# S5 mixer: the first input unit multiplied token block by token block, the last unit's halves in two banks, and the first gate products ahead of the second output turn

## The reference, cut to what matters

```python
def second_block(x, ...):
    for i in range(2):
        h = rmsnorm(x, mix_pre_gain[i])
        m = fox_mixer(h, ...) if i == 0 else s5_mixer(h, ...)
        x = x + rmsnorm(m, mix_post_gain[i])
        h = rmsnorm(x, ffn_pre_gain[i])
        x = x + rmsnorm(swiglu(h, ...), ffn_post_gain[i])

def s5_mixer(h, w_in, ..., d_skip, w_glu, w_out):
    u = h @ w_in                       # 1024 x 1024
    # u -> 64 groups of 16 channels, complex diagonal recurrence over the tokens,
    # in chunks; y = C x, summed over 64 states a group
    y = y + d_skip * u
    y = gelu(y)
    y = y * sigmoid(y @ w_glu)         # 1024 x 1024
    return y @ w_out
```

## Time and profile before

| | us |
|---|---|
| median of 3 runs | 989.36 (989.02 to 989.72) |
| the profiled execution's own time | 988.04 |
| its span | 986.2 |
| PE busy in it | 963.3 (98%) |
| DVE busy | 583.5 (59%) |
| ACT busy | 506.9 (51%) |
| POOL busy | 310.8 (32%) |

### The profile page before, as it was taken

One profiled execution on the slowest core, in us unless ns is written; L12 is line 12 of the kernel. 1 busy time (PEld: TensorE's weight loads), 2 busy tenths in 40 slices (PEclk: granted clock), 3 DMA queues, 4 the chain that ended last, 5 costly groups with the idle time before them and its releaser, 6 DMA issues.

```text
span 986.2 us, 14283 instructions
## 1 busy us (share of the span) xinstructions
PE 963.3 (98%) x5446; PEld 800.2 (81%) x5446; DVE 583.5 (59%) x639; ACT 506.9 (51%) x723; POOL 310.8 (32%) x331
## 2 busy tenths in 40 slices
PE   8999999999999989999999999999989999999997
PEld 6977777888888868888888888888978888888886
DVE  4898875554554456565774545546586755545544
ACT  6855465444443467456654444434456564444332
POOL 5670447999699216763010000000000020000000
PEclk9999999999999999999999999999999999999999
DMA  9842026676776746545446657557946456557551
GB/s 335 271 136 86 1 90 220 224 224 222 264 230 225 223 147 212 162 164 171 129 147 199 187 173 241 185 206 247 381 167 215 128 173 197 185 172 254 172 170 43
DMA packets 133827, 186.79 MB, mean 189 GB/s; under 512 B 5904, under 2 KB 104720, under 8 KB 133264
## 3 DMA queue, kind: packets, MB, share of 16 engines
q1 hardware_dynamic: 109632, 158.28, 49.3%
q10 hardware_dynamic: 24144, 27.81, 8.2%
HBM read 174.54 MB, written 15.73 MB: 193 GB/s over the span
## 4 chain that ended last, share of the span: by engine, by line
PE 91%; DVE 5%; ACT 2%; issue 1%; POOL 0%; DVEq 0%; POOLq 0%; ACTq 0%
PE ps L510 25%; PE ps L482 16%; PE ps L484 16%; PE ps L483 16%; PE ps L1055 2%; PE ps L462 2%; PE ps L464 2%; PE ps L463 2%; PE ps L839 1%; PE ps L1631 1%; PE ps L1074 1%; DVE wlo L422 1%; PE ps L1065 1%; PE ps L621 1%; PE ps L1160 1%
## 5 line engine op out<-in xcount | busy, mean ns | idle before, releaser
L422 DVE TENSOR_TENSOR wlo<-wraw,whi 128x2048 fp32r<-128x2048 f32 x127 | 302.0, 2380 | 293.1 <-ACT whi L416 293.1
L416 ACT ACTIVATE whi<-wraw 128x2048 fp32r<-128x2048 f32 x127 | 243.2, 1915 | 255.4 <-PE ps L484 156.3
L482 PE MATMUL ps<-whi,actH 128*128 128x512 f32 x640 | 258.0, 403 | 6.8 <-DVE wlo L422 5.9
L484 PE MATMUL ps<-whi,actL 128*128 128x512 f32 x640 | 250.2, 391 | 0.0
L483 PE MATMUL ps<-wlo,actH 128*128 128x512 f32 x640 | 249.4, 390 | 0.0
L482 PEld LDWEIGHTS ps<-whi,actH 128*128 128x128 f32 x640 | 120.3, 188 | 33.7 <-DVE wlo L422 6.5
L484 PEld LDWEIGHTS ps<-whi,actL 128*128 128x128 f32 x640 | 120.1, 188 | 26.1
L756 POOL TENSOR_SCALAR ss<-ss 128x1 f32<-128x1 f32 x8 | 1.8, 221 | 436.1 <-ACT sg L726 436.1
L483 PEld LDWEIGHTS ps<-wlo,actH 128*128 128x128 f32 x640 | 120.5, 188 | 22.3
L510 PE MATMUL ps<-whi,gH 128*128 128x512 f32 x248 | 77.8, 393 | 0.0
L510 PE MATMUL ps<-wlo,gH 128*128 128x512 f32 x248 | 76.8, 390 | 0.0
(11 more groups left out here) (452 smaller groups left out, 1573.7 us busy)
## 6 DMA issues: line engine op xcount, KB each, us to landing
wraw<-in_ffn_w_gate SPq DMA_DIRECT2D x44, 512.0 KB, 4.0
wraw<-in_ffn_w_up SPq DMA_DIRECT2D x44, 512.0 KB, 4.9
wraw<-in_ffn_w_down SPq DMA_DIRECT2D x18, 1024.0 KB, 4.9
wraw<-in_fox_w_in SPq DMA_DIRECT2D x16, 1024.0 KB, 5.4
wraw<-in_w_gate SPq DMA_DIRECT2D x22, 512.0 KB, 4.1
wraw<-in_w_up SPq DMA_DIRECT2D x22, 512.0 KB, 5.0
wraw<-in_w_in SPq DMA_DIRECT2D x9, 1024.0 KB, 11.2
wraw<-in_w_down SPq DMA_DIRECT2D x9, 1024.0 KB, 5.0
```

The costliest lines, as they stand in the source:

```text
L416: act.activation(self.high_of(n0), self.wraw[:, n0 % RAW, :], ACT.Copy).then_inc(self.hi_done, 1)
L422: dve.tensor_tensor(self.low_of(n0), self.wraw[:, n0 % RAW, :], self.high_of(n0).bitcast(F32), ALU.subtract).then_inc(self.lo_done, 1)
L482: pe.matmul(out, xh, wh, start=(ka == 0), stop=False)
L484: last = pe.matmul(out, xl, wh, start=False, stop=(ka == KT - 1))
```

## The change

Four places, all in the S5 layer's code:

- The first input unit takes the activations as the stationary operand and the weights as the moving one (`mm_tokens`), first for row block 0, then for row block 1. The turn of `x_res` becomes the row-by-row turn that the feed-forward parts already use (`pe_row_turn`, `act_row_turn`, `dve_row_turn`), and the 40 matmuls on the identity go. The unit's result has tokens on partitions; ACT copies it into `sg`, and PE turns it back with four transposes in the middle of the second unit. Its low part now lies in its raw slot, so the first gate unit's transfer waits for `used` of this unit.
- The fourth input unit puts its first half of features in bank 3 and its second half in bank 0, so that DVE can take the first half while PE computes the second.
- `turn_inputs(0)` turns all of `Vc` first and then all of `Vs`, each behind its own wait.
- The first gate unit's products with the first tile are issued ahead of `turn_outputs(1)`; ACT's gelu table load moves ahead of `states_swapped(3)`, its order around `outputs_out(3)` and DVE's around `yg_low` change.

Semaphores of the first layer's LayerNorm are renamed (`ln_total`), with the same waits.

```diff
-        self.early_low = {f["s"]: early["b"], f["f2.down"] + FT // 2 - 1: early["act"]}
+        self.early_low = {f["f2.down"] + FT // 2 - 1: early["b"]}
...
+    def mm_tokens(self, pe, st, n0, r, bank):
+        pe.wait_ge(self.lo_done, n0 + 1)
+        out = self.ps[:, bank, r * 256:(r + 1) * 256]
+        for k in range(KT):
+            pe.wait_ge(*self.past(st + "_act_ready", KT * r + k + 1))
+            wh, wl = (t[:, k * 256:(k + 1) * 256] for t in (self.high_of(n0), self.low_of(n0)))
+            xh, xl = self.actH[:, k, r * P:(r + 1) * P], self.actL[:, k, r * P:(r + 1) * P]
+            pe.matmul(out, xh, wh, start=(k == 0), stop=False)
+            pe.matmul(out, xh, wl, start=False, stop=False)
+            last = pe.matmul(out, xl, wh, start=False, stop=(k == KT - 1))
+        if r == RT - 1:
+            last.then_inc(self.used, 1)
...
-            m.pe_ffn(pe, "f2", f2_turn, last_units=2, half=lambda: s_first(0), end=lambda: s_first(1))
-            s_rest()
-            for i in range(4):
-                m.mm_features(pe, first["s"] + i, i, ready="s_act_ready" if i == 0 else None,
-                              late=late if i == 0 else None)
+            s_turn = lambda r, part: m.pe_row_turn(pe, "s", "pf0_x_ready", ROWS_HIGH, r, part)
+            m.pe_ffn(pe, "f2", f2_turn, last_units=2, half=lambda: s_turn(0, 0), end=lambda: s_turn(0, 1))
+            m.mm_tokens(pe, "s", first["s"], 0, 0)
+            s_turn(1, 0)
+            s_turn(1, 1)
+            m.mm_tokens(pe, "s", first["s"], 1, 0)
...
+            for i in range(1, 4):
+                if i == 3:
+                    pe.wait_ge(*m.past("ut1", 1))
+                m.mm_features(pe, first["s"] + i, i, middle=tokens_turned if i == 1 else None,
+                              second=0 if i == 3 else None)
...
-            turn_outputs(1)
             n = first["glu"]
             pe.wait_ge(m.lo_done, n + 1)
             for i, k in enumerate(Y_ORDER):
+                if i == 1:
+                    turn_outputs(1)
                 pe.wait_ge(*m.past("yg_act_ready", i + 1))
+                if i == 0:
+                    pe.wait_ge(*m.past("y_out_a", 3))
                 for f in range(2):
-                    o, c = ps[:, 3 * f, 0:TOK], k * 256 + f * P
+                    o, c = ps[:, 2 * f, 0:TOK], k * 256 + f * P
...
-            for i in range(4):
+            for i in range(3):
                 m.act_post_square(act, "pf0", 0, "f2_first", n, i)
+            m.act_row_turn(act, "s", ROWS_HIGH, 0, range(4), MIXPRE + 8)
+            m.act_post_square(act, "pf0", 0, "f2_first", n, 3)
+            m.act_row_turn(act, "s", ROWS_HIGH, 0, range(4, KT), MIXPRE + 8)
             act.wait_ge(*m.past("pf0_squares", 2 * RT))
             act.dma_start(m.RTab[:], m.Rd).then_inc(sem("r_in"), 16)
+            m.act_row_turn(act, "s", ROWS_HIGH, 1, range(KT), MIXPRE + 8)
             act.wait_ge(*m.past("pf0_normed", 2 * RT))
             act.dma_start(m.gb[1][:], io["ffn_post_gain_2"][1:2, :].to_broadcast([P, D])).then_inc(sem("gain1_in"), 16)
-            m.act_turn(act, "s", (4, 5, 6, 7, 2, 3), gain=MIXPRE + 8)
             for r in range(RT):
                 m.act_pre_square(act, "s", "pf0_x_ready", r)
+            act.wait_ge(m.used, n + 1)
+            act.activation(m.sg[:], ps[:, 0, :], ACT.Copy).then_inc(sem("s_tokens"), 1)
...
+            act.activation(m.nmax[:, 0, 0:1], m.halfpi[:], ACT.Gelu_apprx_tanh)
             states_swapped(3)
-            act.activation(m.nmax[:, 0, 0:1], m.halfpi[:], ACT.Gelu_apprx_tanh)
             outputs_out(2)
...
             for i in range(4):
-                dve.wait_ge(m.used, n + i + 1)
                 for h in range(2):
-                    dve.tensor_tensor(m.uT[:, h, :, i, :],
-                                      ps[:, i, h * TOK:(h + 1) * TOK].rearrange("p (c t) -> p t c", t=T),
+                    if i == 0:
+                        dve.wait_ge(*m.past("s_features", 1))
+                    elif (i, h) == (3, 0):
+                        dve.wait_ge(*m.past("features_half", 1))
+                    else:
+                        dve.wait_ge(m.used, n + i + 1)
+                    src = ps[:, 0, 0:TOK] if (i, h) == (3, 1) else ps[:, i, h * TOK:(h + 1) * TOK]
+                    dve.tensor_tensor(m.uT[:, h, :, i, :], src.rearrange("p (c t) -> p t c", t=T),
                                       by_step, ALU.mult).then_inc(sem(f"ut{h}"), 1)
...
-                if i == 3:
-                    yg_low(0)
-                    yg_low(1)
-                if i > 3:
+                if i > 1:
                     yg_low(i - 2)
```

More of the change, by code:

```diff
@@ L106, in resolve @@
             counts["ao"] = counts["fo"] = KT // 2
-            for s in ("f1", "fp", "f2", "f3"):
+            for s in ("f1", "fp", "f2", "s", "f3"):
                 counts[s] = RT * KT
@@ L349, in place @@
             ("gain", self.where["postgain0"]), ("nat", self.where["nat"]), ("c", R0 + 36864), ("a", R0 + 49152),
-            ("b", R0 + 57344), ("d", self.where["Uall"]), ("qt", self.where["qt1"]),
-            ("act", self.where["actL"]))}
+            ("b", R0 + 57344), ("d", self.where["Uall"]), ("qt", self.where["qt1"]))}
         self.junk1 = at("junk1", [P, D], F32, self.where["qn"])
@@ L447, in low_piece, with mm_features @@
                           ALU.subtract).then_inc(done, 1)
-    def mm_features(self, pe, n0, bank, it=0, ready=None, order=range(KT), middle=None, late=None):
-        pe.wait_ge(self.lo_done, n0 + 4 * it + 1)
+    def mm_features(self, pe, n0, bank, order=range(KT), middle=None, second=None):
+        pe.wait_ge(self.lo_done, n0 + 1)
         high, low = self.high_of(n0), self.low_of(n0)
@@ L454, in mm_features @@
             out = self.ps[:, bank, f * TOK:(f + 1) * TOK]
+            if second is not None and f == 1:
+                last.then_inc(self.sem("features_half"), 1)
+                out = self.ps[:, second, 0:TOK]
             for i, k in enumerate(order):
[L456 to L459, removed]
                 c = k * 256 + f * P
@@ L640, in dve_row_turn @@
                .then_inc(self.sem(st + "_act_ready"), 1)
[L642 to L672, removed]
     def pe_spread(self, pe, st, bank):
@@ L1858, in turn_inputs @@
             def turn_inputs(b):
[L1860 to L1865, removed]
+                parts = ((m.Vc, b, 3 + b),) if b > 0 else ((m.Vc, 0, 1), (m.Vs, 4, 3))
+                for src, bank, ready in parts:
+                    pe.wait_ge(*m.past("vc_a", ready))
+                    for q in range(4 * b, 4 * b + 4):
+                        last = pe.transpose(ps[:, bank, (q % 4) * P:(q % 4 + 1) * P], src[:, q, :], idn[:])
                 last.then_inc(sem("v_turned"), 1)
@@ L2286, in _, with yg_gelu, yg_high @@
             outputs_out(1)
+            act.activation(m.nmax[:, 0, 0:1], m.halfpi[:], ACT.Gelu_apprx_tanh)
             states_swapped(3)
-            act.activation(m.nmax[:, 0, 0:1], m.halfpi[:], ACT.Gelu_apprx_tanh)
             outputs_out(2)
-            for i, kt in enumerate(Y_ORDER + (None,)):
-                if i == 2:
-                    outputs_out(3)
-                if kt is not None:
-                    act.wait_ge(*m.past("y_sum", i + 1))
-                    act.activation(m.ygT[:, kt, :], m.ygT[:, kt, :], ACT.Gelu_apprx_tanh).then_inc(sem("gelu"), 1)
-                if i > 0:
-                    act.wait_ge(*m.past("gelu", i))
-                    act.activation(m.actH[:, Y_ORDER[i - 1], :], m.ygT[:, Y_ORDER[i - 1], :], ACT.Copy)\
-                       .then_inc(sem("yg_high_ready"), 1)
+            def yg_gelu(i):
+                yg = m.ygT[:, Y_ORDER[i], :]
+                act.wait_ge(*m.past("y_sum", i + 1))
+                act.activation(yg, yg, ACT.Gelu_apprx_tanh).then_inc(sem("gelu"), 1)
+            def yg_high(i):
+                kt = Y_ORDER[i]
+                act.wait_ge(*m.past("gelu", i + 1))
+                act.activation(m.actH[:, kt, :], m.ygT[:, kt, :], ACT.Copy).then_inc(sem("yg_high_ready"), 1)
+            for i in range(2):
+                yg_gelu(i)
+                yg_high(i)
+            outputs_out(3)
+            for i in range(2, KT):
+                yg_gelu(i)
+                if i > 2:
+                    yg_high(i - 1)
+            yg_high(KT - 1)
             n = first["glu"]
```

27 lines of the change are left out of this document (17 added, 10 removed), and 2 rows, old and new, of the table KINDS.

## The result

The changed kernel took 997.99 us (median of 6 runs, 997.25 to 1000.84), the kernel before 989.54 us beside it. The ratio is 1.0087, 95% interval 1.0073 to 1.0101. My 988.5 us and my range of 986.9 to 989.9 were both wrong.

A forecast was written before the change was run, and what follows sets the result against it. PE was taken to bound the input units, DVE the recurrence. Profiled 988.04 less 0.87 + 0 + 0.3, plus 0.34, gave 987.2; the same 0.83 off the median 989.36 gave 988.5 us, range 986.9 to 989.9.

The forecast's parts named there:

- Part 4: End of the recurrence: first gate products ahead of the second output turn, table load moved earlier; a loss of 0.34 us.
- part 2: Fourth input unit's halves: the wait for `nat` goes, but ACT's split ahead of `Ur` still holds PE's second turn; gain 0.
- Part 1: First input unit, with the row-by-row turn and without fillers: the third input unit begins earlier, a gain of 0.87 us.
- 0.8 us of cover: In the first input unit's term: DVE's low part of the third unit is ready 0.8 us ahead of PE.
- Part 3: First turn of the recurrence: `Vc` turned before `Vs` lets PE start earlier, a gain of 0.3 us.
- the rival on the table load: ACT between `outputs_out(1)` and `states_swapped(3)`: load takes 1.3 us more, gate 1.1 us later; 989.6 us, chance 9%.
- Transfers: Rival: later gate loads delay the first half table, PE waits up to 1 us in the recurrence; 989.5 us, chance 5%.
- The clock: Rival: without 40 filler matmuls PE has gaps between 690.6 and 697, half clock costs 1.5 us; 990.0 us, chance 4%.

The follow-up runs named there:

- the early load: The changed kernel, with the first input unit's low part in its own buffer, so the gate loads are issued early: 988.23 us, ratio 0.999.
- Before with the late load: The kernel before, with only the first gate unit's load held until PE has used the first input unit: 996.52 us, ratio 1.007.

## Why the load was late: rows, not bytes

**Tables in rows of 1 KB**, four pieces each:

```diff
-            act.dma_start(m.RTab[:], m.Rd).then_inc(sem("r_in"), 16)
+            for y in range(4):
+                dst, src = (v.rearrange("p (x y z) w -> p y x (z w)", y=4, z=2)[:, y] for v in (m.RTab[:], m.Rd))
+                act.dma_start(dst, src).then_inc(sem("r_in"), 16)
```

> The changed kernel, with one edit: RTab and OTab are each loaded in four pieces whose rows are 1 KB long, as those of the gate units' loads are; same bytes, same queue, same places. Theory 1a (the DMA engines take turns between the two queues packet by packet, so that 1 KB packets get little beside packets of some 20 KB): the gate load now gets about half of the rate and lands 6 to 12 us after its issue instead of 22; PE's long wait goes, 988 to 991 us. Theory 1b (the load is late by the bytes that are in line ahead of it, whatever their packets): it lands after 18 to 22 us as before, 996 to 999 us.

Half right. The load landed after 8.3 us, as 1a has it. But the kernel became 6 us slower than the changed one: ACT was held while it issued the pieces (`ACTq`: start, us), and PE with it.

```profile
694.45 6.31 ACTq L2218 DMA_DIRECT2D RTab<-R_dram  x4
...
710.35 11.28 ACTq L2236 DMA_DIRECT2D OTab<-O_dram  x4
```

Since ACT fed its queue slowly there, this run alone does not separate the theories.

**Tables in rows of 4 KB**, two pieces each, the same edit with `y=2, z=8`:

> The changed kernel, with one edit: RTab and OTab are each loaded in two pieces whose rows are 4 KB long (32 KB in the changed kernel, 1 KB in the run before this one). Theory 1a (turns packet by packet): the gate load's 1 KB packets get about one part in five beside them, so it lands 12 to 16 us after its issue, between the 22 of the 32 KB rows and the 10 of the 1 KB rows, near 716 to 719 us; PE's wait behind the fourth unit is 0 to 2 us; 988.5 to 991.5 us. If ACT is held for its issues as with 1 KB rows (6 and 11 us there), a part of that comes on top, up to 995. Theory 1b (bytes in line): 20 to 23 us again and 997 to 999 us.

A miss in time: ACT was held for 1.3 us only, but the load took 18.9 us, above my 12 to 16 and short of 1b's 20, and PE still waited 5.67. The times do not decide, the packets do. From the DMA view of stretches in which both queues had work (q10 is ACT's, q1 SP's; packets, MB, share of the engines' time). Changed kernel, 711.5 to 715 us:

```profile
q10 hardware_dynamic: 51, 1.36, 90.6%
q1 hardware_dynamic: 57, 0.06, 4.9%
```

The same kernel, 715 to 721:

```profile
q10 hardware_dynamic: 79, 2.59, 100.3%
q1 hardware_dynamic: 79, 0.08, 3.8%
```

And 722 to 724, when the tables are through:

```profile
q1 hardware_dynamic: 692, 0.69, 102.8%
```

Before with the late load, 703 to 710 (ACT's queue also had the 512 KB of a gain here, in rows of 4 KB):

```profile
q10 hardware_dynamic: 214, 2.29, 78.0%
q1 hardware_dynamic: 256, 0.26, 13.0%
```

Rows of 4 KB, 706 to 711:

```profile
q10 hardware_dynamic: 368, 1.38, 77.5%
q1 hardware_dynamic: 373, 0.38, 24.2%
```

The counts are nearly equal (1 : 1.1, 1 : 1.0, 1 : 1.2, 1 : 1.0) while the bytes stand at 23, 32, 9 and 3.6 to 1, so a share by bytes is excluded. Beside 32 KB rows the load crawls, and most of it moves when ACT's queue is through. The 4 KB run also shows why I missed its time: at 0.38 MB in 5 us, 1 MB takes 13 us, but of the load, issued at 699.62, nothing had moved by 702.5. In the changed kernel too, ACT's queue moved 46 packets from 703.7 to 707 and SP's none. What holds the start of a load for some 3 us is not shown.

The Trainium skill ("DMA: Bandwidth & Descriptors", section "Queues, rings and completion order") says that each engine goes round the queues that have work, a packet at a time. The traces agree, with the profile's packets as the unit: 79 to 79 from 715 to 721.

**Everything in SP's queue**, in the order of need (ACT's two issues go):

```diff
+                    if n == first["glu"]:
+                        sp.wait_ge(*m.past("pf0_squares", 2 * RT))
+                        sp.dma_start(m.RTab[:], m.Rd).then_inc(sem("r_in"), 16)
                     if n == first["glu"] + 2:
+                        sp.wait_ge(*m.past("s_features", 1))
+                        sp.dma_start(m.OTab[:], m.Od).then_inc(sem("o_in"), 16)
```

> The changed kernel, with one edit: SP issues RTab ahead of the first gate unit's load and OTab behind the second's, so that tables and weights stand in one queue; rows stay 32 KB, the gate load's issue stays as late as in the changed kernel. Theory 1a (turns between queues, packet by packet; within one queue in order): RTab lands near 709, the gate loads 3 and 5.5 us behind it at some 400 GB/s, 8 to 10 us after their issue instead of 22; OTab near 726, the first table half near 729. PE's wait of 8.7 us goes; 0 to 1.5 us of wait may be left for the first table half: 987.8 to 989.8 us. Theory 1b (the late load is bytes in line, whatever the queue) would have the gate load no earlier than 719 and 994 us or more.

Confirmed: the same bytes, rows and late issue, but one queue, and the long wait is gone (distance 64.82, the early load has 64.75). What is left is small:

```profile
729.24 0.39 PE L1872 MATMUL ps<-zerob,identb 128*128 128x512 bf16 x1 [0.43 <-DMA wraw<-T_dram]
```

This needs no buffer. By its time alone it would not separate the theories, since `OTab` now stands behind the gate loads, so that fewer bytes are in line with them; it is the packet counts that decide for 1a.

## The clock behind the wait

```diff
+            for _ in range(130):
+                pe.matmul(ps[:, 7, 0:P], m.identb[:], m.identb[:], start=True, stop=True)
             for h in range(2):
                 pe.wait_ge(*m.past(f"ut{h}", 4))
```

> The changed kernel, with one edit: 130 matmuls of 128 columns that produce nothing stand where PE waits 8.7 us behind the fourth input unit (7.8 us by the 0.06 of each of the 40 in the kernel before). It prices the clock apart from the wait. Theory 1: the load is as late as before, but the granted clock stays at 1.00 behind the wait, where it was 0.50 to 0.54 for 10 us; both turns of u (3.68 and 2.15 us) go back to 1.97 and 1.94: 1.7 to 1.9 us faster than the changed kernel, 996.1 us. Rival (the clock falls for another reason, or does not matter): 998 us.

```profile
718.88 7.43 PE L1826 MATMUL ps<-identb 128*128 128x128 bf16 x130
728.00 1.97 PE L1831 MATMUL ps<-ident,nat 128*128 128x128 f32 x16 [1.69 <-DVE nat L2667]
729.97 1.94 PE L1840 MATMUL ps<-ident,Ur 128*128 128x128 f32 x16
```

The load is as late, the granted clock stays at 1.00, both turns have their old length, and the distance is 1.46 us shorter (997.99 to 996.61 by the medians). I said 1.7 to 1.9. The load happened to take 22.23 us here, and the first turn starts 37.93 us behind the third square (at 690.07) instead of 37.71. From the start of that turn to the sigmoid it is 35.22 us instead of 36.90, so the clock by itself costs 1.68.

## Experiments on the parts

**Part 4 undone** (PE, ACT and DVE at the end of the recurrence as before, early load kept).

> The changed kernel with the early gate loads (as in the run with the low part in a buffer of its own), and part 4 undone: table load, second output turn and first gate products as in the kernel before. The traces of the two say so far that part 4 costs 0.15 us at the end of the first gate unit (gain 1.39 ahead of it, 1.24 behind it); my prediction said 0.34. Expected by this: 0.1 to 0.35 us faster than with part 4, 988.0 us. Rival (part 4 is neutral or a gain): the same or up to 0.4 us slower. The total can hardly tell; the distances from the third square do.

The distance is 0.25 us shorter (64.50 against 64.75), so part 4 costs 0.25, against my 0.34.

**High products first.** On that kernel:

```diff
+            with_high(0)
+            turn_outputs(1)
+            for i in range(KT):
+                if i > 0:
+                    with_high(i)
+                last = with_low(i)
```

`with_high` waits for a tile's high part and issues its four products, `with_low` waits for the low part and issues two.

> As the run above (early gate loads, parts 1 to 3, part 4 undone), and in the first gate unit the two products of a tile that need its high part alone stand ahead of the wait for its low part; those of the first tile also ahead of the second output turn. If the end of that unit hangs on the last low parts with six products behind each, as I read it, only two are left behind each: 0.6 to 1.0 us earlier, 987.2 us, ratio 0.997 to 0.9985. Rival (PE's sum decides the unit, or the extra waits cost as much): 988.0 us as the run above.

The sigmoid of the first gate unit, part 4 undone (third square 688.80), then high products first (689.99):

```profile
753.30 0.38 ACT L2305 ACTIVATE sgT<-ps 128x256 f32<-128x256 f32 x1 [0.63 <-PE ps L1929]
```

```profile
754.14 0.38 ACT L2320 ACTIVATE sgT<-ps 128x256 f32<-128x256 f32 x1 [0.19 <-PE ps L1936]
```

64.50 and 64.15: a gain of 0.35, half of what I expected. The unit did not hang on its last low parts alone.

**The second gate unit's split behind `Ur`.**

```diff
-            for i in (3, 4, 5):
+            for i in (3, 4):
                 m.split_high(act, n + i)
...
                    .then_inc(sem("ur_a"), 1)
+            m.split_high(act, n + 5)
```

> The best version so far, with ACT's split of the second gate unit moved behind its two copies of Ur (ahead of Uall). It tests the reason for my gain of 0 in part 2: if that split is what holds the second turn of u, the wait of 0.72 us for Ur ahead of it goes, and comes back larger behind, since ACT's Uall copies are 1.2 to 1.9 us later: by the span 0.4 to 1.2 us slower than the best version. Rival (DVE's second copy of Ur, which ends at the same time, holds the turn as well): the wait stays at 0.6 to 0.7.

```profile
723.29 2.00 PE L1840 MATMUL ps<-ident,Ur 128*128 128x128 f32 x16
725.98 1.95 PE L1851 MATMUL ps<-RTab,Uall 128*32 128x128 f32 x64 [0.69 <-ACT Uall L2258]
```

The wait for `Ur` is gone, so ACT's split does hold it, as my part 2 said; DVE's copy that ends beside it serves the turn's second half. 0.69 us came back at `Uall`, no more: the distance is 0.08 shorter, and my 0.4 to 1.2 slower fell. (It ran only once. Its 990.09 has a third square 2.6 us later than the version above, ahead of the edit.)

**`Ur` by halves.** DVE copies both banks of the first half, ACT both of the second.

```diff
-                    pe.wait_ge(*m.past("ur_a", q // 8 + 1))
-                    pe.wait_ge(*m.past("ur_d", q // 8 + 1))
+                    pe.wait_ge(*m.past("ur_a" if q else "ur_d", 2))
```

> The best version so far, with the four copies of Ur dealt out otherwise: DVE copies both banks of the first half, ACT (busy with the split of the second gate unit until then) both of the second. The second turn then waits for DVE alone, which can start its copies as soon as the first banks are written: 0.3 to 0.5 us earlier, 987.1 us, ratio 0.9965 to 0.9985. Rival (ACT's later copies hold the second half of the turn, or the recurrence's DVE chain passes nothing on): 987.5 us, as the best version.

```profile
719.95 1.29 DVE L2674 COPY Ur<-ps 128x512 f32<-128x512 f32 x2
```

```profile
721.29 2.20 PE L1839 MATMUL ps<-ident,Ur 128*128 128x128 f32 x16
```

PE's wait went from 0.73 to under 0.2, though the turn itself now takes 2.20 us instead of 1.96, with a wait of 0.25 for ACT's later copies ahead of its second half; the distance fell by 0.45. This is the fastest version: 986.51 us, ratio 0.9971.

## Why the prediction was wrong, by its steps

- *Part 1, gain 0.87*: right. The spread ahead of the third unit stands 0.86 us earlier in the version with the early load (707.33 against a third square at 690.47), and 0.84 in the changed kernel. The 0.8 us of cover for the third unit's low part held.
- *Part 2, gain 0*: right, with its reason. The second turn of u comes 0.98 us earlier (721.98 - 690.47 = 31.51, against 721.15 - 688.66 = 32.49), so 0.12 over part 1, behind a wait of 0.72 for `Ur`.
- *Part 3, gain 0.3*: 0.41. DVE's first product of the recurrence starts 1.39 us earlier (36.52 behind the third square against 37.91), 0.98 of it from ahead.
- *Part 4, loss 0.34*: 0.25 against the version without it (0.15 if read as the gain of 1.39 ahead of it that is 1.24 behind it). In the version with the early load, the second output turn starts 0.30 later against what is ahead of it (a gain of 1.39 becomes 1.09), as worked out. The table load began where `outputs_out(1)` ended (740.62 + 0.60; load at 741.24) and the next operation came 1.29 us behind that, so the rival on the table load is out, and nothing here shows the drain that the Trainium skill ("ScalarE: Activation LUTs", section "What ACT_TABLE_LOAD costs") adds.
- The sum of the parts was a gain of 0.83; measured 1.24.
- *Transfers, 5%, 989.5 us*: here the prediction failed. The sum has no term for the moved gate loads, and the rival had at most 1 us for them. They cost 9.86 us (distance 74.61 against 64.75 with the load early). I had the right event and a wrong price, by two steps. "At its 396 GB/s 2 MB are 5.3 us" counts what the loads add to the bytes in line, as if the queues took turns by bytes. Beside the 32 KB rows of `RTab` and `OTab` the first load got 3 to 4% of the bytes, and landed after 22 us where it had taken 6.7. And I looked for the consequence behind the load, at the first table half in the recurrence ("would wait up to 1 us"). It was in front: ACT's split and DVE's low part of that gate unit stand, in program order, ahead of `uT` and `Ur` of the input units, and PE waited 8.74 us for them. My own evidence against the rival, a DMA share of 0.24 in the recurrence, spoke of the wrong stretch; the row that bore on it was 0.96 from 694.60 to 718, where the load was now to run. I also overlooked that the row-by-row turn on ACT moves the issue of both tables 2.0 us back (`RTab` from 691.30 to 697.45 in the two traces, 2.64 and 4.63 us behind the square).
- *The clock, 4%, 1.5 us*: the size came near (1.68), the cause was another. Missing fillers ahead of S5 cost nothing (1.00 from 690 to 722); the long wait did it. That the size fits is luck.

Together, against the version with the early load: the first turn of u starts 8.91 us later (37.71 against 28.80 behind the third square), the clock adds 1.68, and the long wait swallows the 0.72 of waiting for `Ur`. That makes 9.87, where the distances differ by 9.86. Less the 1.24 that the parts gain, it is the loss of 8.62 by distance, 8.45 by the medians.

## What to carry to other kernels

When an edit moves a transfer, price it at its new place: which other queue has work there, and how long that queue's rows are. In this kernel a load of short rows on one queue crawled beside a load of long rows on another. Keeping them in one queue in the order of need, or starting the short-row one first, brought the time back. And look for the cost of a late landing not where the data is used, but at the first instruction of any engine that waits for it: all that stands behind that instruction in program order waits too.

## What the runs showed of the hardware that I had not expected

- Two queues share the DMA engines by packets. 1 MB in 1 KB rows landed after 22.0 us beside 32 KB rows, 18.9 beside 4 KB rows, 8.3 beside 1 KB rows (from a queue that ACT filled slowly), and 6.7 and 7.7 in the kernel before.
- A DMA's issue can hold its engine: 4 MB took ACT 0.34 us to issue with 32 KB rows, 1.3 with 4 KB rows, 6.3 and 11.3 with 1 KB rows, and PE waited up to 7.2 us behind it. The fill of the queue has a part in it: in the version with one queue, SP took 4.41 us to issue the same `OTab` in 32 KB rows behind the two gate loads. How much is due to the number of rows by itself was not tried.
- In the long wait PE's granted clock went to 0.50, and it stayed there until PE had worked for some 3.5 us (some 4.3 in the kernel before with the late load). Matmuls that produce nothing kept the clock at 1.00 through the same wait.
